# Five places reordered and a chunk-major scratch layout in a three-stage fp32 network on one core

## The reference, cut to what matters

```python
def first_block(x, c, ...):
    sh_m, sc_m, gt_m, sh_f, sc_f, gt_f = split(silu(c) @ ada_w + ada_b, 6)
    h = rms_norm(x, mix_pre_g) * (1.0 + sc_m) + sh_m
    m = token_mix(h, w_in, ...)            # conv branch and recurrence, then @ w_out (1024 x 1024)
    x = x + gt_m * rms_norm(m, mix_post_g)
    h = rms_norm(x, ffn_pre_g) * (1.0 + sc_f) + sh_f
    f = channel_mix(h, w_up, ..., w_down)  # 1024 -> 2 * 2816 -> 1024
    return x + gt_f * rms_norm(f, ffn_post_g)

def hybrid_layer(x, w_in, ...):            # called twice
    q, k, v, z_attn, z_ssm, xbc, dt_raw = split(x @ w_in)
    attn = sliding_window_attention(q, k, v, sinks) * silu(z_attn)
    xbc = silu(causal_depthwise_conv(xbc, conv_w, conv_b))
    xs, bm, cm = split(xbc)                # 1024, 256 and 256 channels
    y = ssd_chunked(xs, dt, a, bm, cm)     # 8 chunks of 128 tokens, a state carried from one to the next
    y = y + xs * d_skip
    ssm = gated_rmsnorm(y, z_ssm, ssm_norm_w)
    out = concatenate([attn, ssm]) @ w_out # 2048 x 1024
    return layer_norm(DEEPNORM_ALPHA * x + out, ln_g, ln_b)
```

## Time and profile before

| | us |
|---|---|
| median of three runs | 3173.84 |
| lowest and highest run | 3173.08, 3182.57 |
| profiled execution, own time | 3177.89 |
| its span in the profile | 3176.1 |
| PE busy | 3018.6 |
| DVE busy | 1570.4 |
| ACT busy | 1134.3 |
| POOL busy | 971.5 |

### The profile page before, as it was taken

How to read it: one execution, slowest core, us unless ns; L and a number is a source line. 1 busy time by engine, 2 the same in 40 slices (tenths; PEclk the granted TensorE clock), 3 DMA queues, 4 the chain that set the end, 5 groups by cost and what they waited for, 6 DMA issues and landing times. The chain is left out here.

```text
span 3176.1 us, 50311 instructions
## 1 busy us (share of the span) xinstructions
PE 3018.6 (95%) x21202; PEld 2383.5 (75%) x21202; DVE 1570.4 (49%) x2328; ACT 1134.3 (36%) x1946; POOL 971.5 (31%) x596
## 2 busy tenths in 40 slices
PE   6999689899999999999999999989999999999998
PEld 4887378677888887887877777767778777777677
DVE  4999756444232234334134434389431334434885
ACT  3012433343222122213134434575322344345643
POOL 3442013213333334332233333242123333332421
PEclk8999899899999999999999999999999999999999
DMA  5112400041111111122212113497531122127864
GB/s 217 52 47 71 175 4 4 31 145 40 47 46 53 46 53 40 50 100 95 68 48 84 62 60 106 158 263 191 166 106 54 40 80 84 50 93 239 242 174 149
DMA packets 341388, 304.42 MB, mean 96 GB/s; under 512 B 11296, under 2 KB 300448, under 8 KB 336704
## 3 DMA queue, kind: packets, MB, share of 16 engines
q1 hardware_dynamic: 270016, 240.53, 24.9%
q10 hardware_dynamic: 71168, 60.96, 6.0%
HBM read 244.69 MB, written 54.66 MB: 94 GB/s over the span
## 5 line engine op out<-in xcount | busy, mean ns | idle before, releaser
L2309 PE MATMUL PS<-x_high_sb,w_high_sb 128*128 128x512 f32 x1312 | 530.9, 405 | 0.0
L2309 PE MATMUL PS<-x_high_sb,w_low_sb 128*128 128x512 f32 x1312 | 518.6, 395 | 0.0
L2309 PE MATMUL PS<-x_low_sb,w_high_sb 128*128 128x512 f32 x1312 | 518.0, 395 | 0.0
L2309 PEld LDWEIGHTS PS<-x_high_sb,w_high_sb 128*128 128x128 f32 x1312 | 247.5, 189 | 76.6 <-issue 23.8
L2309 PEld LDWEIGHTS PS<-x_high_sb,w_low_sb 128*128 128x128 f32 x1312 | 247.3, 189 | 57.9
L2309 PEld LDWEIGHTS PS<-x_low_sb,w_high_sb 128*128 128x128 f32 x1312 | 247.8, 189 | 52.4
L2556 DVE CUSTOM_DVE_ANT_0 scores_sb<-PS,attn_raw_sb,sinks_sb 128x256 f32<-128x256 f32 (+1 forms) x256 | 104.5, 464 | 342.4 <-PE PS L2327 342.4
L1743 DVE SCALAR_TENSOR_TENSOR z_sb<-PS,cols_sb,z_sb 128x1023 f32<-128x1023 f32 x88 | 112.7, 1282 | 313.7 <-ACT z_sb L1729 307.8
L378 PE MATMUL PS<-h_high_sb,up_high_sb 128*128 128x512 f32 x672 | 261.4, 389 | 0.0
L378 PE MATMUL PS<-h_low_sb,up_high_sb 128*128 128x512 f32 x672 | 261.4, 389 | 0.0
L378 PE MATMUL PS<-h_high_sb,up_low_sb 128*128 128x512 f32 x672 | 261.4, 389 | 0.0
(11 more groups left out here) (462 smaller groups left out, 6135.4 us busy)
## 6 DMA issues: line engine op xcount, KB each, us to landing
xbc_sb<-w_in SPq DMA_DIRECT2D x80, 512.0 KB, 3.8
wo_raw_sb<-w_up SPq DMA_DIRECT2D x44, 512.0 KB, 3.9
ada_slots_sb<-ada_w SPq DMA_DIRECT2D x16, 1024.0 KB, 6.7
decays_sb<-running_sums SPq DMA_DIRECT2D x16, 1024.0 KB, 9.3
attn_raw_sb<-state_out ACTq DMA_DIRECT2D x32, 512.0 KB, 4.2
attn_raw_sb<-attn ACTq DMA_DIRECT2D x28, 512.0 KB, 6.6
xbc<-staged_sb ACTq DMA_DIRECT2D x24, 512.0 KB, 2.7
xbc_sb<-xbc SPq DMA_DIRECT2D x16, 768.0 KB, 7.2
```

Of the source, the lines that this page charges most:

```text
L2309: last = pe.matmul(PS[:, bank, :], a[:, n % 2, k], b[:, k, cols], start=k == 0 and a is WH and b is HH, stop=k == KT - 1 and a is WL)
```

## The change

1. `in_projection`: POOL computes low parts 0 to 2 before the second weight tile (n == 1) and the other 13 before the third.
2. `out_projection`: with LAST = 3, parts and rests of the last three tiles stand behind squares and gains 0 to 2, and before square and gain 3.
3. `down_projection`: the squares of F stand between the last casts, with a scratch tile of their own. Seven tiles are turned ahead instead of four, each behind a wait for the row tiles it reads.
4. Scratch: shape (chunks, 128, tiles, 128). Loads of the state-space stage and its store become one run of 4 KB per partition (6 KB for xbc), stores of the projection stage become runs of 512 bytes. An attention store becomes two DMAs, and the counts that wait for it double.
5. `state_space_and_mix`: the casts of rounds 3 and 7 stand before `high(a + 1)` and `root(c - 1)`; `invert(c - 1)` stands before `weigh(c + 1)`. At the end of the first layer eight tiles are turned ahead.

```diff
@@ in_projection, POOL
-                if n == 2:
-                    h.gpsimd(pool, range(2 * KT))
+                if n in (1, 2):
+                    h.gpsimd(pool, range(3) if n == 1 else range(3, 2 * KT))
@@ out_projection, ScalarE
-            for q in range(KT):
+            for q in range(KT - LAST):
                 part(KT + q)
...
-            for k in range(G):
+            for k in range(LAST):
                 square(k)
+            for q in range(KT - LAST, KT):
+                part(KT + q)
+            square(LAST)
@@ out_projection, DVE
-            for q in range(KT):
+            for q in range(KT - LAST):
                 rest(KT + q)
...
-            for k in range(G):
+            for k in range(LAST):
                 gain(k)
+            for q in range(KT - LAST, KT):
+                rest(KT + q)
+            gain(LAST)
@@ down_projection, PE
-            for n in range(AHEAD):
+            for n in range(AHEAD_IN_DOWN):
+                pe.wait_ge(s.scaled, AFTER_DOWN[n] + 1)
                 turn_rows(m, pe, X, AFTER_DOWN[n], n)
@@ down_projection, ScalarE
+            act.wait_ge(s.eps, 1)
             for i in range(FT + TT // 2, 2 * FT):
                 high(i)
-            act.wait_ge(s.eps, 1)
-            act.wait_ge(s.moved, TT)
-            act.wait_ge(s.low, 2 * FT)
...
-            for k in range(TT):
-                if k:
-                    act.wait_ge(s.sq, k)
-                nc.scalar.activation(junk, F[:, k], ACT.Square, accum_out=ss[:, k:k + 1]).then_inc(s.sq, 1)
+                k = i - FT - TT // 2
+                if k < TT:
+                    act.wait_ge(s.moved, k + 1)
+                    if k:
+                        act.wait_ge(s.sq, k)
+                    nc.scalar.activation(junk[:], F[:, k], ACT.Square, accum_out=ss[:, k:k + 1]).then_inc(s.sq, 1)
@@
-AHEAD = 4
+AHEAD_IN_DOWN = 7
@@ TurnedIn (self.ahead in place of AHEAD in tensor and scalar)
-            x = TurnedIn(m, HH, HL, AFTER_LAYER if i else AFTER_DOWN)
+            x = TurnedIn(m, HH, HL, *((AFTER_LAYER, KT) if i else (AFTER_DOWN, AHEAD_IN_DOWN)))
@@ projections_and_attention, stores on ACT's queue
-                dst = (xbc_d if job[0] == "xbc" else gate_d)[job[1]]
-                act.dma_start(dst, ST[:, slot[job]]).then_inc(stage[slot[job]], 16)
+                dst = (xbc_d if job[0] == "xbc" else gate_d)[:, :, job[1]].rearrange("c p t -> p c t")
+                act.dma_start(dst, ST[:, slot[job]].rearrange("p (c t) -> p c t", c=TT)).then_inc(stage[slot[job]], 16)
...
-                act.dma_start(attn_d[2 * g:2 * g + 2].rearrange("k p t -> p k t"),
-                              AT[:, 2 * (g % 2):2 * (g % 2) + 2]).then_inc(s.stored, 16)
+                for i in range(2):
+                    act.dma_start(attn_d[:, :, 2 * g + i].rearrange("c p t -> p c t"),
+                                  AT[:, 2 * (g % 2) + i].rearrange("p (c t) -> p c t", c=TT)).then_inc(s.stored, 16)
@@ state_space_and_mix, SP and ACT's queue
-                sp.dma_start(XB[:, c % 2], chunk(xbc_d[:, :, cols(c)])).then_inc(xb_in[c % 2], 16)
+                sp.dma_start(XB[:, c % 2], xbc_d[c]).then_inc(xb_in[c % 2], 16)
...
-                sp.dma_start(ZS[:], chunk(gate_d[:, :, cols(c)])).then_inc(s.z_in, 16)
+                sp.dma_start(ZS[:], gate_d[c]).then_inc(s.z_in, 16)
...
-                sp.dma_start(chunk(y_d[:, :, cols(c)]), YT[:, c % 2]).then_inc(y_out[c % 2], 16)
+                sp.dma_start(y_d[c], YT[:, c % 2]).then_inc(y_out[c % 2], 16)
...
-                    act.dma_start(AA[:, u % 2], chunk((y_d if state else attn_d)[:, :, cols(k)])).then_inc(aa_in[u % 2], 16)
+                    act.dma_start(AA[:, u % 2], (y_d if state else attn_d)[k]).then_inc(aa_in[u % 2], 16)
@@ state_space_and_mix, PE
-                for n in range(AHEAD):
+                for n in range(KT):
+                    if n == TT // 2:
+                        pe.wait_ge(s.added, UNITS)
                     turn_rows(m, pe, X, AFTER_LAYER[n], n)
@@ state_space_and_mix, ScalarE
                     square(c - 1)
+                    for i in range(WS + 4, WS + KT) if c == 3 else range(WS + KT + 4, WS + 2 * KT) if c == 7 else ():
+                        cast(i)
                     high(a + 1)
                     root(c - 1)
-                    for i in range(WS + 4, WS + KT) if c == 3 else range(WS + KT + 4, WS + 2 * KT) if c == 7 else ():
-                        cast(i)
@@ state_space_and_mix, DVE
+                if c:
+                    invert(c - 1)
                 if c and c + 1 < TT:
                     weigh(c + 1)
-                if c:
-                    invert(c - 1)
@@ second_layer
-    scratch = lambda name, tiles: m.nc.dram_tensor(f"{name}_{i}", (tiles, P, T), F32, kind="Internal").ap()
+    scratch = lambda name, tiles: m.nc.dram_tensor(f"{name}_{i}", (TT, P, tiles, P), F32, kind="Internal").ap()
```

More of the change, by code:

```diff
@@ L1877, in down_projection @@
         W2 = alloc(m, ctx, "down_parts", [P, 2, NH], F32R)
+        junk = alloc(m, ctx, "squares", [P, NH])
         W0 = [parts[:].rearrange("p q (a b) n -> p q a (b n)", a=2) for parts in W0]
@@ L2001, in _ @@
                 act.wait_ge(s.sq, TT + k)
-                nc.scalar.activation(junk, PS[:, k, :], ACT.Square, accum_out=ss[:, TT + k:TT + k + 1]
+                nc.scalar.activation(junk[:], PS[:, k, :], ACT.Square, accum_out=ss[:, TT + k:TT + k + 1]
                                      ).then_inc(s.sq, 1)
@@ L2070, with __init__ @@
 class TurnedIn:
-    def __init__(self, m, HH, HL, banks):
-        self.m, self.HH, self.HL, self.banks = m, HH, HL, banks
+    def __init__(self, m, HH, HL, banks, ahead):
+        self.m, self.HH, self.HL, self.banks, self.ahead = m, HH, HL, banks, ahead
         self.s = phase(m, "turned high low")
@@ L2083, in tensor @@
         m, s = self.m, self.s
-        for n in range(max(half * KT, AHEAD), half * KT + KT):
+        for n in range(max(half * KT, self.ahead), half * KT + KT):
             held = [i for i in range(n) if self.banks[i] == self.banks[n]]
@@ L2094, in scalar @@
         for n in range(2 * KT):
-            if n >= AHEAD:
-                act.wait_ge(self.s.turned, n - AHEAD + 1)
+            if n >= self.ahead:
+                act.wait_ge(self.s.turned, n - self.ahead + 1)
             self.m.nc.scalar.copy(self.HH[self.at(n)], self.m.PS[:, self.banks[n], :]).then_inc(self.s.high, 1)
@@ L2283, in _ @@
             for c in range(2):
-                sp.dma_start(land.XB[:, c], xbc_d[:, :, c * P:(c + 1) * P].rearrange("k p t -> p k t")
-                             ).then_inc(land.xb_in[c], 16)
-            sp.wait_ge(s.stored, 16 * (KVH - 1))
-            sp.wait_ge(land.half_stored, 16)
+                sp.dma_start(land.XB[:, c], xbc_d[c]).then_inc(land.xb_in[c], 16)
+            sp.wait_ge(s.stored, 32 * (KVH - 1))
+            sp.wait_ge(land.half_stored, 32)
             sp.wait_ge(s.biased, TT * (KVH - 1))
-            sp.dma_start(land.AA[:, 0], attn_d[:, :, 0:P].rearrange("k p t -> p k t")).then_inc(land.aa_in[0], 16)
+            sp.dma_start(land.AA[:, 0], attn_d[0]).then_inc(land.aa_in[0], 16)
             sp.wait_ge(s.scored, N)
@@ L2293, in _ @@
             sp.wait_ge(s.biased, N)
[L2294 removed]
+            sp.dma_start(land.AA[:, 1], attn_d[1]).then_inc(land.aa_in[1], 16)
         @block.tensor
@@ L2426, in store @@
             def store(job):
-                dst = (xbc_d if job[0] == "xbc" else gate_d)[job[1]]
-                act.dma_start(dst, ST[:, slot[job]]).then_inc(stage[slot[job]], 16)
+                dst = (xbc_d if job[0] == "xbc" else gate_d)[:, :, job[1]].rearrange("c p t -> p c t")
+                act.dma_start(dst, ST[:, slot[job]].rearrange("p (c t) -> p c t", c=TT)).then_inc(stage[slot[job]], 16)
             def store_attention(g):
                 act.wait_ge(s.gated, TT * (g + 1))
-                act.dma_start(attn_d[2 * g:2 * g + 2].rearrange("k p t -> p k t"),
-                              AT[:, 2 * (g % 2):2 * (g % 2) + 2]).then_inc(s.stored, 16)
+                for i in range(2):
+                    act.dma_start(attn_d[:, :, 2 * g + i].rearrange("c p t -> p c t"),
+                                  AT[:, 2 * (g % 2) + i].rearrange("p (c t) -> p c t", c=TT)).then_inc(s.stored, 16)
             def store_last_attention(part):
-                g, at = KVH - 1, slice(part * NH, (part + 1) * NH)
+                g, half = KVH - 1, slice(part * TT // 2, (part + 1) * TT // 2)
                 act.wait_ge(s.gated, TT * g + (part + 1) * TT // 2)
-                act.dma_start(attn_d[2 * g:2 * g + 2, :, at].rearrange("k p t -> p k t"),
-                              AT[:, 2 * (g % 2):2 * (g % 2) + 2, at]).then_inc(
-                                  (land.half_stored, land.rest_stored)[part], 16)
+                for i in range(2):
+                    act.dma_start(attn_d[half, :, 2 * g + i].rearrange("c p t -> p c t"),
```

(8 more changed lines are left out.)

3 lines of the change are left out of this document (removed).

## The result

The changed kernel takes 3156.5 us in the median of four runs (3152.3 to 3156.7), the kernel before 3176.5 us beside it: ratio 0.9934, 95% interval 0.992 to 0.9949, 20 us faster. Later, on another occasion, it took 3150.9 us against 3173.0, ratio 0.9931 (0.9918 to 0.9943). The forecast was 3148 us, 3134 to 3164. The time lies inside, and the direction is right. The kinds of gain are partly others than forecast, though. On the first occasion the first rival had the better number (3156 us), for a reason that the runs refute; the later gain of 22.1 us lies nearer to the forecast's 25.8 than to that rival's 17.5.

A forecast was written before the change was run, and what follows sets the result against it. PE, busy 95% of the span, and its pauses were taken to bound the kernel. The terms -0.5 + 7.4 + 1.0 + 19.3 - 1.4 = 25.8 us, off 3173.8 us, gave 3148.0 us, range 3134 to 3164.

The forecast's parts named there:

- the first rival: Reordering alone works: small packets cost nothing, inverse first gives nothing; 17.5 us gained, 3156 us, chance 0.2.
- 1. start: Wait for low part 1 goes, but PE starves at later parts and its clock may rise later: 0.5 us lost.
- 2. out projection: Last casts run while PE multiplies; its 6.0 us wait and the low clock behind go: 7.4 us (5.5 to 8).
- 3. down projection, squares: Squares move to ScalarE's idle time, so DVE's last addition comes sooner: 2.4 us gained.
- 3. seven tiles ahead: At the first layer's boundary, the first product waits for POOL's split anyway; more products at low clock: 1.4 us lost.
- 4. rounds 0 and 1: State-space stages: inverse first, given a lead by the layout, ends PE's wait for the inverse root: 8.3 us (0 to 10.1).
- 4. rounds 2 to 5 (round 3's casts): State-space stages: casts start sooner, but ScalarE waits for the fourth piece, delaying DVE: 3 us gained (-3 to +12.4).
- 4. rounds 6 and 7 (round 7's casts): State-space stages: casts start 2.4 us sooner, shrinking PE's waits for weight pieces: 8 us gained (0 to 11.4).
- 5. eight tiles ahead: First to second layer: first product waits for POOL's split, later clock costs 1.4 us (0 to 2.5).
- signs of being wrong: First, PE still pauses in round 1; second, waits for the pieces stay; third, ScalarE waits for stores.
- the waits only change places: Rival: casts cost in rounds 3 and 7 what they gain, DVE bounds first rounds; 6.5 us remain, 3167 us, chance 0.08.
- the inverse's term: State-space stages: reciprocal before the decays' multiplication, with the layout giving DVE's lead: 8.3 us gained (0 to 10.1).

The follow-up runs named there:

- x5: The changed kernel with four tiles turned ahead at both boundaries, as before the change, the squares staying where the change put them: 3148.0 us.
- x9: The changed kernel with the old start, four tiles ahead, two of round 3's casts in front, chunk 5 loaded early: 3138.4 us, ratio to before 0.9894.
- x10: x9 with the reciprocal of the root behind the multiplication of the decays again: 3138.7 us, ratio to before 0.9892.
- x1: The kernel before with the new scratch layout alone, every order of work as before: 3166.8 us, ratio to before 0.9972.
- x2: The changed kernel with the old scratch layout, all reorderings kept: 3167.4 us, ratio to before 0.9964.
- x3: The changed kernel with round 3's casts behind the high part and the root again, round 7's still in front: 3151.7 us.

## Why the prediction came out as it did

By its own terms, from the stretches (means where there are several profiles):

| part | forecast | measured |
|---|---|---|
| 1. start | -0.5 | -0.6 or -2.4 to -3.4 |
| 2. out projection | +7.4 | +7.3 |
| 3. down projection, squares | +2.4 | +2.2 |
| 3. seven tiles ahead | -1.4 | -1.4 |
| 4. rounds 0 and 1 | +8.3 | +11.0 |
| 4. rounds 2 to 5 (round 3's casts) | +3 | -4.9 |
| 4. rounds 6 and 7 (round 7's casts) | +8 | +8.8 |
| 5. eight tiles ahead | -1.4 | -1.9 |
| layout outside these places | 0 | +1.5 between the stages, +1.1 at the end |

Out projection: 96.1 and 97.3 us with the old order, 89.4 in the mean of eleven profiles with the new. Part 3: 827.0 us in the mean without it, 826.3 with seven tiles, 824.9 with four and the squares moved (x5, x9, x10). Rounds: the mean of the four profiles. The layout's +1.5 is 671.8 - 670.3 (x1), one profile each; the changed order gives the same, 673.5 us with the old layout (x2) and 671.9 us in the mean with the new. With the start at -1.7 in the mean of its eight profiles the terms add up to 22 us, against 20.0 and 22.1 in the medians. That the sum came so near to 25.8 us is partly luck: rounds 2 to 5 were 7.9 us worse than forecast, rounds 0 and 1, round 7 and the layout elsewhere 6.1 us better.

**Right** were the out projection, the squares, the turned tiles and round 7, each within 1 us and by the mechanism named. That the first product waits for POOL's split, and that turning ahead takes away work at the low clock, is shown by x5. The last addition came 4 us behind PE's last product, as forecast. Of the signs of being wrong, the first and the third did not come: PE does not pause in round 1 of either layer (a chunk wait of 1.8 us opens round 2 of the second), and ScalarE waits for no store of the projection stage. The second came in part: the waits for the pieces fell to 1.5 us, but waits for the chunk took their place.

**Wrong** was the step "Round 3: ... I count 1.5 us per layer, 3 us (-3 to +12.4)". It lost 4.9 us, past its own low end. The chain up to DVE was named rightly: ScalarE blocks on the fourth piece, the high part moves (by 7 us: it came at 2127.2, and ScalarE turned to the casts at 2119.9; forecast some 6). Two things were not counted. SP's queue holds the next xbc chunk behind the same four piece loads; before the change PE's pauses for the pieces covered that (it waited 1.7 us for chunks in all, and x3, where these pauses are back, has 1.8 us). And no order alone shortens these rounds: they took 176.0 us before, 176.4 with the layout alone, 176.9 with the inverse last, 177.3 with two casts first and 180 to 182 in the changed order, or with round 3's casts back. Each order chooses which wait shows and how much low clock follows. Only x9 and x10, which cure the supply on both queues, get under 176 us. The rival "the waits only change places" had that for rounds 2 to 5; it was wrong for rounds 0, 1 and 7.

**Mis-sized** was the layout. It was given to the inverse's term as its condition (8.3 us together). Alone it is worth 7.4 us in rounds 0 and 1, as DVE comes 3 us sooner to everything behind; the inverse first adds 2 to 4 us there and gives 4 us back later. The bound of 10.1 us counted PE's wait for the inverse alone, and 11.0 us were gained. DMA: Bandwidth & Descriptors (Specifications) of the Trainium skill has 512 bytes as enough for line rate, by which the layout would give nothing. The runs speak against using it so for one queue beside another: x1 changes nothing but the lengths of the runs and the split of the attention stores, and saves 7.2 us in these stages. Which of the loads brings it was not tried one by one; ScalarE's waits speak for those of the attention.

**The clock at the boundaries.** The cost of 1.4 us was right at the first and 0.5 us short at the second. TensorE: Matmul & The Clock Gate (part 4, PE-mode transpose) of the Trainium skill says that transposes do not count as busy in the same way, by which x5 would have gained nothing on the changed kernel. It gained 1.2 and 1.9 us, and its clock rose 1.3 us after the first product, not 5; in x10 it rose before the first product. Here they counted.

The start's loss has the size forecast in half of the profiles; in the others the clock comes back some 5 us later, which the range of 1.5 us did not hold. The forecast had the later pause, but put its price at 0.5 us, and did not see that the clock, up sooner than before, would fall behind it. Why it comes back at 53 us in one profile and at 59 in another stays open.

## What to carry to other kernels

Where several engines are close behind PE, moving work in front of a wait helps only if what it needs has arrived. Before moving it, look up when its input lands and what stands behind it on the queue that brings it: here four casts in front of late pieces gained nothing, while two of them in front, with the load of the next chunk taken out from behind those pieces, gained 7 us. Two late supplies that cover each other must be cured together: tried one at a time, the cures gave 2.3 and 0.9 us and both looked hardly worth having.

When the total scatters more than a part is worth, cut each profile at landmarks of the busiest engine and compare stretches; an unedited stretch that varies shows where the noise sits.

## What was not expected of the hardware

- The layout, with loads in runs of 4 to 6 KB in place of 512 bytes, brought 7.2 us with no order changed, though the bytes are the same and the longest landing of an attention load fell only from 15.7 to 10.4 us. In the window of the earlier trace rows ACT's queue now moved 118 packets with 0.42 MB, where it had moved 349 with 0.18 MB (q10; SP's queue, q1, carries other loads in this window than before):

```profile
q1 hardware_dynamic: 674, 0.68, 76.0%
q10 hardware_dynamic: 118, 0.42, 30.6%
```

- The opposite rows, stores in runs of 512 bytes, cost nothing that shows: they landed after 3.2 us in the median, 2.7 before. With the layout alone the stretch that holds the first projection stage is 0.9 us longer, the one that holds the second 1.5 us shorter; the changed kernel against x2 shows the same signs (0.4 us longer, 1.6 us shorter).
- The same program start led to two different clocks, 1.8 us and more apart in the length of the in projection, in eight profiles of seven kernels. Only the changed kernel was profiled twice, both times with the clock that comes back late, so no single kernel was seen with both.
